# A gated recurrence and an attention of eight heads, laid between the matmuls of the projection before and the output after

## The chip, the cores and the metric

One core of a Trainium2 chip runs the whole program, once. TensorE multiplies, VectorE and ScalarE work on elements, GpSimd makes constants and issues small transfers, and SyncE issues the weight transfers. The metric is device microseconds of one launch, as the median of several runs.

## The reference, cut to what matters

Two transformer blocks of two layers each run over 256 tokens of width 1024, in float32. The change touches the first layer's mixer alone:

```
proj = hn @ w_in                       # 1024 -> 2568 columns
xr, yr, q, k, v, f_logit = split(proj) # 512 each, f_logit 8
xc = causal_conv(xr, width 4); r, i = sigmoid(block_diag(xc))
a = exp(-8 * r * softplus(-lam)); u = sqrt(1 - a*a) * (i * xc)
y_a = scan(h = a*h + u) * gelu(yr)
c = cumsum(log_sigmoid(f_logit + f_b))
y_b = causal_softmax(q k^T / 8 + c_i - c_j) v     # 8 heads of 64
h = h + concat(y_a, y_b) @ w_out
```

## The kernel before

All products of weights run as three float32r matmuls (high by high, high by low, low by high). A weight chunk of 128 x 1024 words lands in one of six slots of `raw_ring`; ScalarE copies its rounded high part (`split_hi`, L1263), VectorE subtracts for the low part (`split_lo`, L1699). `ahead(c)` on either engine splits up to three chunks (LEAD) beyond chunk c. A slot is reused once TensorE counts `chunk_used`, and a raw slot once `lo_ready` has passed. Activations stand in XHI and XLO, with 8 blocks of 128 rows.

The projection has 18 units, in the order of EV_COLS: sixteen "col" units (128 columns of the projection, 24 matmuls of 256 tokens), one "row" unit of 512 columns (V) and one of 8 (the forget logits); a row unit has 48 matmuls. `unit` waits for `bank_free` of the unit before last. VectorE evicts every unit.

Then the parameter rows, which GpSimd has loaded with 59 small transfers, are turned into columns, and `even_mixer` runs by itself: convolution on VectorE, gates on TensorE, sigmoid, exponential, tanh and square root on ScalarE, the scan on VectorE; then 16 attention units, unit v being head v // 2 and row block v % 2. In a unit TensorE makes scores (L875, L877), VectorE adds the bias and takes the maximum (L2054, L2056), ScalarE takes the exponential (L1490), VectorE scales (L2065, L2066), TensorE turns the probabilities (L888), ScalarE copies them (L1483) and TensorE multiplies by V (L894). Then `output` runs eight weight rows (L605), 12 matmuls of 512 columns each, and VectorE adds the residual (L1951).

Each engine executes its instructions in the order of the text; engines wait for each other by semaphores alone. The hybrid mixers of the second block (from about 1820 us) are already laid between column units.

## Time and profile before

| | |
|---|---|
| median of 3 runs | 2790.12 us |
| the three runs | 2780.39, 2792.97, 2790.12 us |
| profiled execution: time, span | 2793.78 us, 2792.0 us |
| mean granted TensorE clock | 0.942 of 2.4 GHz |
| busy share of the span: TensorE, VectorE, ScalarE, GpSimd | 93%, 69%, 52%, 2% |

The profile comes from one execution. Busy time counts instructions in execution, and idle time is given with the instruction that released the engine. A granted clock of 1.00 is 2.4 GHz for TensorE and 0.50 is 1.2 GHz.

### The profile page before, as it was taken

How to read it: one execution, taken by the hardware profiler on the slowest of the kernel's cores; microseconds unless marked ns; L12 is line 12 of the kernel's file. 1: busy time of each engine (PE TensorE's matmuls, PEld its weight loads, DVE VectorE, ACT ScalarE, POOL GpSimd, SP SyncE). 2: the span in 40 equal slices, each digit the busy share in tenths (PEclk: the TensorE clock that was granted, in tenths of full speed). 3: DMA queues.
4: the chain of work that ended last, by engine and by line, in shares of the span. 5: the costliest groups of instructions: out<-in, count | busy, mean ns of one | idle time of the engine just before them, and what ended most of it. 6: DMA issues, size and time to landing. Idle time of an engine off the chain costs nothing.

```text
span 2792.0 us, 40605 instructions
## 1 busy us (share of the span) xinstructions
PE 2600.0 (93%) x15264; PEld 2274.8 (81%) x15264; DVE 1940.5 (69%) x2674; ACT 1459.3 (52%) x1837; POOL 64.2 (2%) x137
## 2 busy tenths in 40 slices
PE   8589999669999999999999989989899899889998
PEld 8359997458888888888888779978799899787897
DVE  5445554448989898998999965578755555687654
ACT  4334442337777777777777743442443443523433
POOL 7000000000000000000000000000000000000000
PEclk9669998679999999999999999989999999989999
DMA  8026554119999999999999965621466556423463
GB/s 238 11 69 187 187 152 151 38 53 346 362 354 355 364 356 351 356 369 347 356 364 356 359 188 186 183 84 62 132 186 187 159 181 188 121 68 105 152 186 107
DMA packets 481892, 597.22 MB, mean 214 GB/s; under 512 B 21882, under 2 KB 313154, under 8 KB 481760
## 3 DMA queue, kind: packets, MB, share of 16 engines
q1 hardware_dynamic: 478048, 589.47, 62.7%
q0 software_dynamic: 3712, 6.00, 0.7%
q8 instruction: 81, 1.33, 0.2%
q14 instruction: 51, 0.42, 0.0%
HBM read 594.35 MB, written 1.05 MB: 213 GB/s over the span
## 4 chain that ended last, share of the span: by engine, by line
PE 88%; DVE 9%; ACT 2%; issue 1%; DMA 0%; SPq 0%; DVEq 0%; ACTq 0%
PE bank L622 23%; PE bank L779 23%; PE bank L805 11%; PE bank L634 11%; PE bank L585 6%; PE bank L582 2%; PE bank L605 2%; PE bank L848 2%; PE bank L1204 1%; PE bank L790 1%; DVE arena L2281 1%; PE bank L1020 1%; PE bank L726 1%; PE bank L950 0%; PE bank L877 0%
## 5 line engine op out<-in xcount | busy, mean ns | idle before, releaser
L1699 DVE TENSOR_TENSOR wlo_ring<-raw_ring,whi_ring 128x1024 fp32r<-128x1024 f32 x1122 | 1319.6, 1220 | 116.8 <-ACT whi_ring L1263 106.1
L1263 ACT CAST whi_ring<-raw_ring 128x1024 fp32r<-128x1024 f32 x1122 | 1141.3, 1052 | 290.3 <-DMA raw_ring<-in_od_exp_w_dram 155.8
L622 PE MATMUL bank<-xhi,whi_ring 128*128 128x256 f32 x1760 | 499.7, 284 | 0.4 <-DVE xlo L1756 0.4
L622 PE MATMUL bank<-xhi,wlo_ring 128*128 128x256 f32 x1760 | 499.0, 284 | 0.0
L622 PE MATMUL bank<-xlo,whi_ring 128*128 128x256 f32 x1760 | 499.0, 284 | 0.0
L622 PEld LDWEIGHTS bank<-xhi,whi_ring 128*128 128x128 f32 x1760 | 338.0, 192 | 4.7 <-issue 0.9
L622 PEld LDWEIGHTS bank<-xlo,whi_ring 128*128 128x128 f32 x1760 | 338.0, 192 | 3.9
L622 PEld LDWEIGHTS bank<-xhi,wlo_ring 128*128 128x128 f32 x1760 | 338.0, 192 | 0.0
L1792 DVE TENSOR_TENSOR hid<-sil,bank 128x256 f32<-128x256 f32 x110 | 46.4, 422 | 400.6 <-ACT sil L1324 400.6
L1324 ACT ACTIVATE sil<-bank 128x256 f32<-128x256 f32 x110 | 42.3, 385 | 499.1 <-PE bank L622 499.1
L779 PE MATMUL bank<-whi_ring,xg0hi 128*128 128x512 f32 x448 | 180.5, 403 | 1.2 <-issue 1.2
L779 PE MATMUL bank<-whi_ring,xg1hi 128*128 128x512 f32 x448 | 180.1, 402 | 0.0
L779 PE MATMUL bank<-whi_ring,xg1lo 128*128 128x512 f32 x448 | 177.5, 396 | 0.0
L779 PE MATMUL bank<-whi_ring,xg0lo 128*128 128x512 f32 x448 | 177.5, 396 | 0.0
L779 PE MATMUL bank<-wlo_ring,xg1hi 128*128 128x512 f32 x448 | 177.4, 396 | 0.0
L779 PE MATMUL bank<-wlo_ring,xg0hi 128*128 128x512 f32 x448 | 177.2, 396 | 0.0
L585 PE MATMUL bank<-xhi,whi_ring 128*128 128x256 f32 x496 | 150.7, 304 | 1.6 <-DVE xlo L1756 1.1
L585 PE MATMUL bank<-xlo,whi_ring 128*128 128x256 f32 x496 | 144.8, 292 | 0.0
L585 PE MATMUL bank<-xhi,wlo_ring 128*128 128x256 f32 x496 | 144.5, 291 | 0.0
L805 PE MATMUL bank<-whi_ring,hidhi 128*128 128x512 f32 x448 | 139.3, 393 | 1.4 <-DVE hidlo L1900 1.4
L805 PE MATMUL bank<-whi_ring,hidlo 128*128 128x512 f32 x448 | 138.6, 391 | 0.0
L805 PE MATMUL bank<-wlo_ring,hidhi 128*128 128x512 f32 x448 | 138.1, 390 | 0.0
(488 smaller groups left out, 3907.6 us busy)
## 6 DMA issues: line engine op xcount, KB each, us to landing
raw_ring<-in_od_exp_w_dram SPq DMA_DIRECT2D x672, 512.0 KB, 5.5
raw_ring<-in_ffn_w_gate_dram SPq DMA_DIRECT2D x88, 512.0 KB, 3.9
raw_ring<-in_ffn_w_up_dram SPq DMA_DIRECT2D x88, 512.0 KB, 5.5
raw_ring<-in_ffn_w_down_dram SPq DMA_DIRECT2D x88, 512.0 KB, 5.4
raw_ring<-in_ev_ffn_w_dram SPq DMA_DIRECT2D x66, 512.0 KB, 5.3
raw_ring<-in_w_in_dram SPq DMA_DIRECT2D x42, 512.0 KB, 4.0
raw_ring<-in_od_w_in_dram SPq DMA_DIRECT2D x24, 512.0 KB, 4.6
raw_ring<-in_ev_w_in_dram SPq DMA_DIRECT2D x20, 512.0 KB, 6.5
```

The source lines that it names most:

```text
L582: last = mm(row_bank(q, n, t), x[:, kt, t * P:(t + 1) * P], w[:, kk, :], start=st and (n > 256 or t == 0), stop=sp_, skip_group_check=True)
L585: last = mm(BANK[q % 2][:, 0:S], w[:, kk, :], x[:, kt, :], start=st, stop=sp_)
L605: last = mm(YB[t][h][:, :], x[:, kt, t * P:(t + 1) * P], w[:, h * 512:(h + 1) * 512], start=(kt == 0 and a == 0), stop=(kt == KT - 1 and a ...
L622: last = mm(BANK[qb][:, half * S:half * S + n], w[:, kt, :], x, start=(kt == 0 and a == 0), stop=(kt == KT - 1 and a == 2))
L634: last = mm(pair[h][:, :], x[:, b, t * P:(t + 1) * P], w[:, h * 512:(h + 1) * 512], start=(start and a == 0), stop=(stop and a == 2), skip ...
L779: last = mm(bank[:, :], x[:, kt, slots], w[:, kk, :], start=(kt == 0 and a == 0), stop=(kt == KT - 1 and a == 2))
L805: last = mm(BANK[4 + h][:, :], x[:, j * P:(j + 1) * P], w[:, h * 512:(h + 1) * 512], start=(g == 0 and j == 0 and a == 0), stop=(g == GROU ...
L848: last = mm(BANK[4 + b][:, (2 * j + t) * P:(2 * j + t + 1) * P], H[:, t, kt * P:(kt + 1) * P], DIAG[:, t, :], start=True, stop=True)
L1263: nc.scalar.copy(WHI[:, slot, 0:n], RAW[:, slot, 0:n]).then_inc(s["hi_ready"], 1)
L1324: af(SIL[:, b, 0:n], BANK[b][:, 0:n], ACT.Silu).then_inc(s["silu_ready"], 1)
L1699: V_.tensor_tensor(WLO[:, slot, 0:n], RAW[:, slot, 0:n], WHI[:, slot, 0:n].bitcast(F32), ALU.subtract)\
L1792: V_.tensor_tensor(HID[:, b, 0:n], SIL[:, qb, 0:n], BANK[qb][:, S:S + n], ALU.mult)\
```

## The change

The 8-column and the 512-column unit come first, then the four of XR, four of YR, and Q and K in turns. `even_mixer` now holds the projection and the output. On TensorE the sums of the forget gates stand after unit 5, the gates after unit 9, and the 16 attention units each follow a half of units 14 to 17 (steps 0 to 7) or a half of an output weight row (`out_part`, steps 8 to 15); the last rows follow. Values of unit v stand one step later. ScalarE evicts V, YR (with Gelu in the same operation), Q and K, and makes the high part of XHI; VectorE evicts the logits and XR, and does its recurrence operations between attention steps. GpSimd loads the rows that this mixer needs first, waits for them, and loads the others after; the constants are made in two parts.

The diff, cut to its core and shifted left by eight columns (Q's separate scaling, the old Gelu operations and the old loops leave):

```diff
-EV_COLS = [("col", P)] * 16 + [("row", 512), ("row", 8)]
+EV_XR, EV_YR, EV_Q, EV_K, EV_V, EV_FL = 0, 512, 1024, 1536, 2048, 2560
+EV_COLS = [("row", 8, EV_FL), ("row", 512, EV_V)] + [("col", P, x + P * i) for x in (EV_XR, EV_YR) for i in range(4)] \
+    + [("col", P, x + P * i) for i in range(4) for x in (EV_Q, EV_K)]
...
+FIRST_LOADS = sum(tile == 0 for tile, _ in row_at.values()) + 16 + 1
...
+    def load_rows(loads):
+        for dst, src in loads:
+            pool.dma_start(dst, src).then_inc(s["loads_done"], 16)
+    load_rows(row_loads[:FIRST_LOADS - 17])
+    pool.dma_start(FB[:, :], A["ev_f_b"].broadcast_to([P, 8])).then_inc(s["loads_done"], 16)
...
     link(nc.gpsimd.memset(ONES[:, :], 1.0))
     link(nc.gpsimd.memset(UPPER[:, :], 1.0))
+    link(nc.gpsimd.memset(CAUSAL[:, :], 0.0))
+    link(nc.gpsimd.memset(SEL[:, :, :], 1.0))
+    select(UPPER[:, :], ALU.is_ge, 0.0, [[1, P]], 0, -1)
+    select(SEL[:, :, :], ALU.is_equal, 0.0, [[1, 8], [0, P]], 0, -1)
+    nc.gpsimd.affine_select(out=CAUSAL[:, P:2 * P], in_=CAUSAL[:, P:2 * P], compare_op=ALU.is_ge, fill=NEG, base=0,
+                            pattern=[[-1, P]], channel_multiplier=1).then_inc(s["consts_ready"], 1)
+    pool.wait_ge(s["consts_ready"], 1)
+    pool.wait_ge(s["loads_done"], 16 * FIRST_LOADS)
+    load_rows(row_loads[FIRST_LOADS - 17:])
...
+    def even_mixer(pr, ou):
...
+        u(0)
+        u(1)
+        pe.wait_ge(s["loads_done"], 16 * FIRST_LOADS)
+        turn_columns(0, 1)
+        for k in range(2, 6):
+            u(k)
+        pe.wait_ge(s["consts_ready"], 1)
+        pe.wait_ge(s["small_ready"], 1)
...
+        mm(BANK[3][:, 8:16], UPPER[:, :], lf[:, 1, :], start=False, stop=True).then_inc(s["cum_ready"], 1)
+        for k in range(6, 10):
+            u(k)
+        pe.wait_ge(s["cols_ready"], 1)
         pe.wait_ge(s["conv_ready"], 1)
         for w, b in ((GA, 4), (GX, 6)):
...
         last.then_inc(s["gates_mm"], 1)
...
+        for k in range(10, 13):
+            u(k)
+        pe.wait_ge(s["loads_done"], 16 * N_LOADS)
+        pe.wait_ge(s["consts_ready"], 2)
+        pe.wait_ge(s["sig_ready"], 8)
+        turn_columns(1, 3)
+        u(13)
...
+        def out_part(kt, t):
+            c_ = ou["c0"] + kt
+            if t == 0:
+                wait(pe, "lo_ready", c_ + 1)
+                pe.wait_ge(s["x_ready"], x_at + kt + 1)
+            wh, wl = WHI[:, c_ % RING, :], WLO[:, c_ % RING, :]
+            for a, (x, w) in enumerate(((XHI, wh), (XHI, wl), (XLO, wh))):
+                for h in range(2):
+                    last = mm(YB[t][h][:, :], x[:, kt, t * P:(t + 1) * P], w[:, h * 512:(h + 1) * 512],
+                              start=(kt == 0 and a == 0), stop=(kt == KT - 1 and a == 2))
+            if t == TT - 1:
+                last.then_inc(s["chunk_used"], 1)
+            elif kt == KT - 1:
+                last.then_inc(s["y_ready"], 1)
...
+        def turn_probs(v):
+            t = v % 2
+            pe.wait_ge(s["probn_ready"], v + 1)
+            wait(pe, "probt_copied", v - 1 if v <= 8 else v)
+            bank = BANK[4 + t] if v < 8 else BANK[1]
...
+        def values(v):
...
+            pe.wait_ge(s["probt_copied"], v + 1)
+            if v == 12:
+                pe.wait_ge(s["x_ready"], x_at + 7)
+            bank = BANK[6 + h // 2] if v < 8 else BANK[0]
...
+        pe.wait_ge(s["cols_ready"], 2)
         scores(0)
         scores(1)
-        pe.wait_ge(s["sig_ready"], 8)
-        for u in range(16):
-            h, t = u // 2, u % 2
-            o = 64 * (h % 2)
-            pe.wait_ge(s["probn_ready"], u + 1)
-            wait(pe, "probt_copied", u - 1)
-            for b in range(t + 1):
-                last = tr(BANK[u % 2][:, b * P:(b + 1) * P], PR[:, u % 2, b * P:(b + 1) * P], IDENT[:, :])
-            last.then_inc(s["probt_ready"], 1)
-            if u + 2 < 16:
-                scores(u + 2)
-            pe.wait_ge(s["probt_copied"], u + 1)
-            for b in range(t + 1):
-                last = mm(BANK[4 + h // 2][o:o + 64, t * P:(t + 1) * P], V[:, b, h * 64:(h + 1) * 64],
-                          PT[:, u % 2, b, :], start=(b == 0), stop=(b == t))
-            last.then_inc(s["pv_ready"], 1)
+        for v in range(16):
+            if v < 8:
+                u(14 + v // 2, v % 2 * KT // 2, (v % 2 + 1) * KT // 2)
+            else:
+                if v == 8:
+                    pe.wait_ge(s["probt_copied"], 8)
+                if v == 12:
+                    pe.wait_ge(s["evhi_ready"], 6)
+                out_part((v - 8) % 4, (v - 8) // 4)
+            turn_probs(v)
...
+    def even_mixer(pr, ou):
...
+        def evict(u, dst, func, scale=1.0):
+            act.wait_ge(s["chunk_used"], c0 + u + 4)
+            act.wait_ge(s["bank_free"], q0 + u)
+            af(dst, BANK[(q0 + u) % 2][:, 0:S], func, scale=scale).then_inc(s["bank_free"], 1)
+        for i in range(5):
+            ahead(c0 + i)
+        act.wait_ge(s["chunk_used"], c0 + 5)
+        act.wait_ge(s["bank_free"], q0 + 1)
+        for t in range(TT):
+            last = nc.scalar.copy(V[:, t, :], row_bank(q0 + 1, 512, t))
+        last.then_inc(s["bank_free"], 1)
+        ahead(c0 + 5)
+        ahead(c0 + 6)
         act.wait_ge(s["spx_ready"], 1)
         af(SPE[:, :], SPN[:, :], ACT.Exp).then_inc(s["spe_ready"], 1)
+        ahead(c0 + 7)
+        ahead(c0 + 8)
+        for i in range(4):
+            ahead(c0 + 9 + i)
+            evict(6 + i, YR[:, i, :], ACT.Gelu_apprx_tanh)
...
         act.wait_ge(s["gates_mm"], 1)
...
+        ahead(c0 + 13)
+        evict(10, Q[:, 0, :], ACT.Copy, 64 ** -0.5)
...
         for i in range(4):
             af(AE[:, i, :], RG[:, i, :], ACT.Exp, scale=SPR[:, i:i + 1]).then_inc(s["aexp_ready"], 1)
+        ahead(c0 + 14)
+        evict(11, K[:, 0, :], ACT.Copy)
+        for i in range(4):
             af(TH[:, i, :], RG[:, i, :], ACT.Tanh, scale=SPS[:, i:i + 1]).then_inc(s["aexp_ready"], 1)
+        ahead(c0 + 15)
+        evict(12, Q[:, 1, :], ACT.Copy, 64 ** -0.5)
+        ahead(c0 + 16)
         act.wait_ge(s["root_in"], 1)
         af(TH[:, :, :], TH[:, :, :], ACT.Sqrt).then_inc(s["root_ready"], 1)
...
+        evict(13, K[:, 1, :], ACT.Copy)
+        ahead(c0 + 17)
+        def hi(kt, src):
+            nc.scalar.copy(XHI[:, kt, :], src).then_inc(s["evhi_ready"], 1)
...
+        exps(0)
+        exps(1)
+        for v in range(16):
+            if v < 8 and v % 2:
+                ahead(c0 + 17 + v // 2)
+                u = 14 + v // 2
+                if u % 2 == 0:
+                    evict(u, Q[:, u // 2 - 5, :], ACT.Copy, 64 ** -0.5)
+                else:
+                    evict(u, K[:, u // 2 - 5, :], ACT.Copy)
+            if v == 5:
+                act.wait_ge(s["pv_ready"], 4)
+                nc.scalar.copy(PVS[:, 0, :], BANK[6][:, 0:S])
+            if v == 8:
+                act.wait_ge(s["lru_ready"], 1)
+                hi(0, YR[:, 0, :])
+            copy(v)
+            if v + 2 < 16:
+                exps(v + 2)
+            if v == 7:
+                act.wait_ge(s["chunk_used"], c0 + 21)
+            if v == 8:
+                for kt in range(1, 4):
+                    hi(kt, YR[:, kt, :])
+                act.wait_ge(s["pv_ready"], 8)
+                nc.scalar.copy(PVS[:, 1, :], BANK[7][:, 0:S])
+                ahead(oc)
+            if v == 9:
+                act.wait_ge(s["lru_ready"], 1)
+                hi(4, PVS[:, 0, :])
+                hi(5, PVS[:, 1, :])
+                ahead(oc + 1)
+            if v == 10:
+                ahead(oc + 2)
+            if v == 12:
+                act.wait_ge(s["pv_ready"], 12)
+                hi(6, BANK[0][:, 0:S])
+            if v in (13, 14, 15):
+                ahead(oc + v - 10)
+        ahead(oc + 6)
+        act.wait_ge(s["pv_ready"], 16)
+        hi(7, BANK[0][:, 0:S])
+        ahead(oc + 7)
+        load_root()
...
+    def even_mixer(pr, ou):
...
+        def evict(u, dst):
+            ahead(c0 + u + 3)
+            dve.wait_ge(s["chunk_used"], c0 + u + 4)
+            dve.wait_ge(s["bank_free"], q0 + u)
+            V_.tensor_copy(dst, BANK[(q0 + u) % 2][:, 0:S]).then_inc(s["bank_free"], 1)
+        ahead(c0)
+        dve.wait_ge(s["chunk_used"], c0 + 1)
+        V_.tensor_copy(flat_(FL), BANK[q0 % 2][:, 0:16]).then_inc(s["bank_free"], 1)
...
+        for i in range(1, 5):
+            ahead(c0 + i)
+        dve.wait_ge(s["cols_tp"], 1)
+        V_.tensor_copy(COLS[:, 0, :], BANK[6][:, 0:P]).then_inc(s["cols_ready"], 1)
+        dve.wait_ge(s["cols_ready"], 1)
...
+        evict(2, XR[:, 0, 4:S + 4])
+        evict(3, XR[:, 1, 4:S + 4])
+        ahead(c0 + 7)
         dve.wait_ge(s["spe_ready"], 1)
         log1p(SP[:, :], SPE[:, :], SPP[:, :], SPR[:, :], SPS[:, :])
...
+        evict(4, XR[:, 2, 4:S + 4])
+        evict(5, XR[:, 3, 4:S + 4])
+        dve.wait_ge(s["bank_free"], q0 + 6)
         for j in range(4):
+            ahead(c0 + 9 + j)
...
+        ahead(c0 + 14)
         dve.wait_ge(s["sig_ready"], 8)
         link(V_.tensor_tensor(flat_(IG), flat_(IG), flat_(XC), ALU.mult))
+        ahead(c0 + 15)
+        dve.wait_ge(s["aexp_ready"], 4)
+        link(V_.tensor_tensor(flat_(RG), flat_(AE), flat_(AE), ALU.mult))
+        dve.wait_ge(s["cols_tp"], 2)
+        for t in (1, 2):
+            last = V_.tensor_copy(COLS[:, t, :], BANK[6 - t][:, 0:P])
+        last.then_inc(s["cols_ready"], 1)
+        dve.wait_ge(s["cols_ready"], 2)
         dve.wait_ge(s["aexp_ready"], 8)
-        link(V_.tensor_tensor(flat_(RG), flat_(AE), flat_(AE), ALU.mult))
         V_.scalar_tensor_tensor(flat_(TH), flat_(RG), 1.0, flat_(TH), ALU.add, ALU.mult)\
             .then_inc(s["root_in"], 1)
...
+        ahead(c0 + 16)
+        ahead(c0 + 17)
...
+        def lo(kt, src):
+            dve.wait_ge(s["evhi_ready"], kt + 1)
+            V_.tensor_tensor(XLO[:, kt, :], src, XHI[:, kt, :].bitcast(F32), ALU.subtract)\
+                .then_inc(s["x_ready"], 1)
+        logits(0)
+        logits(1)
+        for v in range(16):
+            normed(v)
+            if v + 2 < 16:
+                logits(v + 2)
+            if v == 1:
+                dve.wait_ge(s["root_ready"], 1)
+                link(V_.tensor_tensor(flat_(IG), flat_(IG), flat_(TH), ALU.mult))
+            if v == 2:
+                for i in range(4):
+                    last = V_.tensor_tensor_scan(XC[:, i, :], AE[:, i, :], IG[:, i, :], 0.0, ALU.mult, ALU.add)
+                link(last)
+            if v == 3:
+                dve.wait_ge(s["bank_free"], q0 + 10)
+                V_.tensor_tensor(flat_(YR), flat_(YR), flat_(XC), ALU.mult).then_inc(s["lru_ready"], 1)
+                dve.wait_ge(s["lru_ready"], 1)
+            if v < 8 and v % 2:
+                ahead(c0 + 17 + v // 2)
+            if v == 7:
+                lo(0, YR[:, 0, :])
+            if v == 8:
+                for kt in range(1, 4):
+                    lo(kt, YR[:, kt, :])
+                ahead(oc)
+            if v == 9:
+                lo(4, PVS[:, 0, :])
+                lo(5, PVS[:, 1, :])
+                ahead(oc + 1)
+            if v == 10:
+                ahead(oc + 2)
+            if v == 12:
+                lo(6, BANK[0][:, 0:S])
+            if v in (13, 14, 15):
+                ahead(oc + v - 10)
+        ahead(oc + 6)
+        lo(7, BANK[0][:, 0:S])
+        ahead(oc + 7)
```

## Rows read from the trace of the kernel before

**Rows 1.** Windows by stage: width, busy of each engine, granted clock, DMA share.

```profile
13.80:78.00 64.20, 63.19 (x481) 61.13 (x482) 36.15 (x49) 22.95 (x27) 37.37 (x75) 0.99 0.76 215
78.00:117.40 39.40, 10.35 (x40) 7.29 (x39) 22.76 (x58) 16.63 (x28) 0.00 (x0) 0.59 0.00 1
117.40:176.60 59.20, 48.80 (x128) 25.71 (x128) 21.39 (x73) 15.63 (x50) 0.00 (x0) 0.50 0.00 0
176.60:200.60 24.00, 23.53 (x92) 19.25 (x92) 9.97 (x11) 7.79 (x9) 2.01 (x3) 0.87 0.66 200
```

**Rows 2.** Chain that ended last, first 260 us: start, length, what.

```profile
18.08 43.45 PE bank L585 x360
...
200.57 1.23 DVE h L1951
```

**Rows 3.** Waits between 78 and 177 us: who for whom, total, times, longest.

```profile
DVE arena L2054 <- PE bank L877: 35.7, 14, 3.1
PE bank L888 <- DVE arena L2066: 23.0, 15, 16.0
```

**Rows 4.** Timeline of TensorE over one head: start, busy, instruction.

```profile
122.58 0.69 PE L888 MATMUL bank<-ident,arena 128*128 128x128 f32 x2 [0.60 <-DVE arena L2066]
123.20 1.22 PE L875 MATMUL bank<-arena 64*128 64x256 f32 x2
...
125.49 1.11 PE L894 MATMUL bank<-arena 128*64 128x128 f32 x4
126.99 0.47 PE L888 MATMUL bank<-ident,arena 128*128 128x128 f32 x1 [0.38 <-DVE arena L2066]
...
128.83 0.69 PE L894 MATMUL bank<-arena 128*64 128x128 f32 x2
```

**Rows 5.** Windows of the projection's last two units, columns as in rows 1.

```profile
61.50:72.30 10.80, 10.80 (x50) 8.91 (x49) 4.05 (x5) 3.16 (x3) 0.00 (x0) 1.00 0.63 238
72.30:78.00 5.70, 5.70 (x50) 5.70 (x49) 2.42 (x3) 0.00 (x0) 0.00 (x0) 0.93 0.31 90
```

**Rows 6.** Timeline of TensorE after the recurrence's gates.

```profile
102.11 0.70 PE L875 MATMUL bank<-arena 64*128 64x256 f32 x2
102.73 0.48 PE L877 MATMUL bank<-arena,sel 8*128 8x256 f32 x1
```

**Rows 7.** Costliest groups of the page: busy, mean ns, idle before.

```profile
L1699 DVE TENSOR_TENSOR wlo_ring<-raw_ring,whi_ring 128x1024 fp32r<-128x1024 f32 x1122 | 1319.6, 1220 | 116.8 <-ACT whi_ring L1263 106.1
L1263 ACT CAST whi_ring<-raw_ring 128x1024 fp32r<-128x1024 f32 x1122 | 1141.3, 1052 | 290.3 <-DMA raw_ring<-in_od_exp_w_dram 155.8
```

**Rows 8.** Timeline of VectorE in recurrence and attention.

```profile
87.97 5.09 DVE L2022 SCALAR_TENSOR_TENSOR arena<-arena,cols 128x256 f32<-128x256 f32 x12
...
111.74 2.44 DVE L2043 TENSOR_TENSOR_SCAN arena<-arena 128x256 f32<-128x256 f32 x4
...
121.39 0.35 DVE L2054 SCALAR_TENSOR_TENSOR arena<-bank,arena,causal 128x128 f32<-128x128 f32 x1 [2.07 <-PE bank L877]
121.78 0.29 DVE L2056 TENSOR_REDUCE arena<-arena 128x1 f32<-128x128 f32 x1
...
122.17 0.35 DVE L2066 TENSOR_SCALAR arena<-arena 128x256 f32<-128x256 f32 x1
```

**Rows 9.** Timeline of ScalarE in recurrence and attention.

```profile
99.14 3.02 ACT L1466 ACTIVATE arena<-bank,cols 128x256 f32<-128x256 f32 x8 [15.10 <-PE bank L857]
...
118.11 0.40 ACT L1490 ACTIVATE arena<-arena 128x128 f32<-128x128 f32 x1 [3.72 <-DVE arena L2056]
```

**Rows 10.** Windows in the later mixer that is woven already.

```profile
1867.00:1869.00 2.00, 0.50 (x5) 0.29 (x3) 1.39 (x3) 0.00 (x0) 0.00 (x0) 1.00 0.07 22
1869.00:1871.00 2.00, 0.00 (x0) 0.00 (x0) 1.93 (x5) 0.00 (x0) 0.00 (x0) 1.00 0.00 0
1873.00:1875.00 2.00, 2.00 (x13) 1.76 (x12) 0.88 (x2) 0.00 (x0) 0.00 (x0) 0.50 0.60 166
```

**Rows 11.** Timeline of GpSimd's transfers.

```profile
29.58 4.14 POOL L456 DMA_DIRECT2D arena<-in_ev_gx_w_dram  x8
```

More of the change, by code:

```diff
@@ L257, in build @@
         AMX, ASUM, AREC = c(16), c(16), c(16)
+        PVS = c(2, S)
         c = Carve()
@@ new lines, in scores @@
+                def scores(v):
+                    h, t = v // 2, v % 2
+                    o, n = 64 * (h % 2), (t + 1) * P
+                    wait(pe, "logit_ready", v - 1)
+                    wait(pe, "bank_free", pr["q0"] + 12 + 2 * (h // 2))
+                    mm(BANK[2 + v % 2][:, 0:n], Q[o:o + 64, h // 2, t * P:(t + 1) * P], K[o:o + 64, h // 2, 0:n],
+                       start=True, stop=False)
+                    mm(BANK[2 + v % 2][:, 0:n], SEL[:, h, :], NCT[:, 0:n], start=False, stop=True)\
+                        .then_inc(s["score_ready"], 1)
@@ L898, in odd_mixer @@
+                out_part(4, 0)
+                values(15)
+                out_part(4, 1)
+                for kt in range(5, KT):
+                    for t in range(TT):
+                        out_part(kt, t)
             def odd_mixer():
@@ L1215, in _ @@
             turn_norm()
-            project(EV_PROJ)
-            pe.wait_ge(s["consts_ready"], 1)
-            pe.wait_ge(s["loads_done"], 16 * N_LOADS)
-            for t in range(3):
-                last = tr(BANK[5 + t][:, 0:P], ROWS[:, t, :], IDENT[:, :])
-            last.then_inc(s["cols_tp"], 1)
-            pe.wait_ge(s["cols_ready"], 1)
-            even_mixer()
-            output(EV_OUT)
+            even_mixer(EV_PROJ, EV_OUT)
             turn_norm()
@@ new lines, in exps @@
+                def exps(v):
+                    n = (v % 2 + 1) * P
+                    act.wait_ge(s["logit_ready"], v + 1)
+                    wait(act, "probt_ready", v - 1)
+                    af(PR[:, v % 2, 0:n], LG[:, v % 2, 0:n], ACT.Exp, bias=AMX[:, v:v + 1],
+                       accum_out=ASUM[:, v:v + 1]).then_inc(s["prob_ready"], 1)
+                exps(0)
[37 more added lines that the diff above has]
+                        ahead(oc + v - 10)
@@ L1644, in _ @@
             gain("norm_mix0")
-            project(EV_PROJ)
-            act.wait_ge(s["cols_ready"], 1)
-            even_mixer()
-            output(EV_OUT)
+            even_mixer(EV_PROJ, EV_OUT)
             norm()
@@ L2068, in even_mixer, with normed @@
-                for p in range(4):
-                    dve.wait_ge(s["pv_ready"], 4 * p + 4)
-                    split_x(BANK[4 + p][:, 0:S], 4 + p, 5 + p, 1)
+                def normed(v):
+                    n = (v % 2 + 1) * P
+                    dve.wait_ge(s["prob_ready"], v + 1)
+                    link(V_.reciprocal(AREC[:, v:v + 1], ASUM[:, v:v + 1]))
+                    V_.tensor_scalar(PR[:, v % 2, 0:n], PR[:, v % 2, 0:n], AREC[:, v:v + 1], None, ALU.mult)\
+                        .then_inc(s["probn_ready"], 1)
@@ L2472, in _ @@
             gain("norm_mix0")
-            project(EV_PROJ, ev_dest)
-            dve.wait_ge(s["cols_tp"], 1)
-            for t in range(3):
-                last = V_.tensor_copy(COLS[:, t, :], BANK[5 + t][:, 0:P])
-            last.then_inc(s["cols_ready"], 1)
-            dve.wait_ge(s["cols_ready"], 1)
-            even_mixer()
-            output(EV_OUT)
+            even_mixer(EV_PROJ, EV_OUT)
             residual(EV_OUT)
```

122 lines of the change are left out of this document (45 added, 77 removed).

## The prediction

> **What bounds the kernel now.** I read the windows by stage first, because the change touches only the first 200 us. The stretch from 13.8 to 200.6 us has four stages [rows 1]: the projection's 18 units, where TensorE works 63.2 of 64.2 us at a granted clock of 0.99; the recurrence (78.0 to 117.4), where it works 10.35 of 39.4 us at 0.59; the attention (117.4 to 176.6), 48.8 of 59.2 us at 0.50; the output, 24.0 us at 0.87. The chain that ended last runs through the projection's matmuls and leaves this layer with VectorE's residual sum at 200.57 [rows 2]. Everything after 200.6 keeps its code, so the kernel's time moves by what 200.57 moves.
>
> The waits of the middle stretch show why TensorE is slow there [rows 3]: VectorE waits 35.7 us in 14 times for scores, TensorE 23.0 us for normalised probabilities (16.0 of it the first). The engines hand one tile round. One head takes 7.4 us (59.2 over 8 [rows 1]) and contains 4.02 us (second row block: 122.58 to 126.60) plus 2.53 us (first: 126.99 to 129.52) of TensorE work, 6.55 us, all at the lower clock [rows 4]. So two things can be won: the waits, if TensorE has other matmuls, and the half clock, if that keeps it granted at full (2.4 GHz instead of 1.2).
>
> **The work that stays.** Nothing large is removed. The projection's units keep 63.2 us of TensorE [rows 1]; a 512-column unit is 10.8 us, the 8-column one 5.7 us [rows 5], and a column unit 24 matmuls of 0.121 us (43.45 us for 360 [rows 2]), 2.9 us. The output at full clock: its window has 24 us at mean 0.87, which is 6.2 us at half and the rest at full; 23.5 us less the 3.1 lost is 20.4 us, 1.28 us for each of 16 new half rows. Attention at full clock: a pair for 256 score columns takes 0.62 us at full (102.11 to 102.73 [rows 6]) and 1.15 at half (two pairs, 123.20 to 125.49 [rows 4]), a ratio of 0.54. Transposes and values have no row at full clock; bounds are 0.5 (the clocks' ratio) and 1.0 of their low-clock time, and I take 0.54, from the matmul beside them in the same head. So 8 x 6.55 x 0.54 = 28.3 us (26.2 to 52.4). Gates, sums and column turns: 10.35 less about 2.0 for the first scores, 8.3 us at mixed clock, 4.9 if all were full (8.3 x 0.59); I take 6.4. Sum of TensorE work: 63.2 + 6.4 + 28.3 + 20.4 = 118.3 us.
>
> **Waits before the first probabilities: 7.9 us.** A split of a weight chunk costs ScalarE 1.05 and VectorE 1.22 us [rows 7]; both queues are executed in order, so each split stands in front of attention or recurrence work.
> - Convolution: four column units hide it. Its 16 operations take 6.5 us (12 in 5.09 [rows 8]) and stand between four splits of which each follows a Gelu eviction on ScalarE, so it can end only after the split that follows unit 8, plus 1.22 and 1.7: about 1.5 us after unit 9.
> - Column turns, second part: TensorE has four column units and two turns after the gates, 12.0 us. ScalarE in that time does sigmoids 3.0 [rows 9], splits, evictions, exponentials and a tanh group; VectorE's split 18 ends about 12.9 us after the gates, then one product (1.2) and two copies (0.5): 14.6. TensorE waits 2.5 us for cols_ready 2.
> - First probabilities: after it, VectorE has a product and two splits, then logits, exponential and scaling, 7.3 us, against scores 0 and 1 and a half unit, 3.4 us: 3.9 us of wait.
>
> **The sixteen steps: 22 us of waits.** TensorE's order in a step is half unit (1.44) or half row (1.28), turn, scores(v+2), values(v-1). From scores(v+2) to the turn of v+2 the chain is logits 0.6 or 0.9 (0.35 + 0.29 at 128 columns), exponential 0.4 plus its sum read (0.6 to 0.7), scaling 0.35 plus a reciprocal, 0.5 [rows 8, 9]: about 2.1 us, against some 6 us of TensorE's work in the two steps between. Bare, the weave has slack. The waits come from what VectorE has in front of normed(v). Steps 0 to 7: 0.9 at step 2 (product 1.2), 1.5 at step 3 (four scans 2.44 [rows 8]), 2.1 at step 4 (product and split), 0.9 at step 6 (split): 5.4. Steps 8 to 15, where three queues take turns at XHI, XLO and the splits: at 8, 2.3 (logits(9), exponential, then hi(0) on ScalarE and lo(0) on VectorE); at 9, 1.5 and 2.2; at 10, 3.6; at 11, 2.2; at 13, 0.7; at 14, 2.9; at 15, 1.1: 16.5. The largest as the pattern: from the end of scores(11), logits 0.9, exponential 0.7, hi(4) and hi(5) 0.7, ScalarE's split 1.05, VectorE's 1.22, normed(10) 0.5 and handovers are 5.3 us; TensorE has values(8) and a half row, 1.7. The smaller ones go the same way: at 9, the four parts of XHI and XLO, 0.4 us each, and one split on both queues stand before normed(9), while TensorE has one half row; at 14 and 15 a split on both queues stands before normed. Together 22 us; bounds 0 (all hidden) and about 44, where each wait is doubled by the other queue.
>
> **The clock: 10 us.** The 8-column unit moves from last to first. In its old place its 5.7 us window averages 0.93 [rows 5], so the clock fell 4.9 us after it began; only 0.8 us was lost then. Now the 512-column unit stands behind it. Low for as long as in the output stage (6.2 us, above) costs 3.1, with the tail of the unit itself 3.8 us (bounds 0 and 5.7 + 3.1). In the steps, the later mixer, which is woven in this way already, shows what a pause does: its window 1867 to 1869 has 0.5 us of matmuls, the next none, both at 1.00, and 1873 to 1875 is full of matmuls at 0.50 [rows 10]. Two of my waits (3.9 and 3.6) are of that size; two low stretches like the output's cost 6.2 us (bounds 0 and what rival 2 gives).
>
> **Moved to other queues, at nothing.** GpSimd issues a transfer each 0.52 us (8 in 4.14 [rows 11]). In front of TensorE's first parameter wait now stand 15 rows, 1 bias and 16 gate blocks: 32 x 0.52 from 2.5 us is 19 to 20 us; the wait is after unit 1, beyond 30 us. The 27 left follow and are wanted only after unit 12. The cover gone, each microsecond late is one of the kernel's. Evictions of YR, Q and K go to ScalarE at 0.33 to 0.4 us each, beside matmuls; the separate scaling of Q and Gelu's four operations leave. SyncE's order of chunks changes only within the projection, and weights of 2 KB rows come first, so the 0.8 us wait near 17.3 us should go (in the 1.0 us idle of [rows 1]; not counted).
>
> **Sum.** 13.8 + 118.3 + 7.9 + 22.0 + 3.8 + 6.2 = 172.0 us for the end of the output, against 200.6: 28.6 us less. The profiled execution took 2793.8 us (span 2792.0), so it becomes 2765; it lies 3.7 above the median of the three runs, so from 2790.1 I predict 2761.5, rounded to 2762.
>
> **Rivals.**
> 1. *Tighter than I count.* The waits of steps 8 to 15 shrink, since work that waits is not late for two reasons at once, and no low stretch follows. For it: the later mixer stays at 1.00 in most windows with such gaps. Against: in-order queues leave no slack at steps 9 and 10. 38 to 48 us less: about 2747.
> 2. *The clock stays low through the sixteen steps.* Attention with 48.8 of 59.2 us busy was never granted more than half [rows 1]. For it: that row; against: now half of TensorE's time is the dense matmuls beside which the clock was full. Work of the steps at half: 52.4 + 23.0 (eight half units) + 20.5 (eight half rows) = 96 us, some 4 of waits, 10.2 of rows left: 110. My sum has 85 from the first turn on: 26.2 of attention (the first two scores are before it), 10.1 of half units, 20.4, 22.0 and 6.2. 25 of the 28.6 us are given back: about 2787.
> 3. *Slower.* As 2, but the waits remain beside the low clock (22 instead of 4) and the last rows are low too (20.4): 138 against 85, 53 us more, 24 slower than before: about 2815. It decides once the steps lose 43 us against my sum.
> 4. *The parameters land late*, or the weave fails to cover at all: price 1 for 1, no row speaks for it.
>
> The Trainium skill (TensorE: Matmul & The Clock Gate, section "HAM oscillation — how this bites in real kernels") speaks against this change: it tells of bursts of matmuls with pauses between, after each of which the array starts again at the low clock. By that rule every step would be like the old attention, and the time would be rival 2's. The trace agrees for one long pause [rows 10] and no row shows a weave of attention.
>
> **How the numbers follow.** Forecast (20 to 37 us less) 0.59; rival 1 0.13; between forecast and rival 2 (14 to 20 less) 0.11; rival 2 (within 14) 0.13; rival 3 and late parameters 0.04. 0.5% is 14 us, about what can be told from no change here (the three runs spread 12.6 us). Faster 0.83, same 0.13, slower 0.04. The range 2746 to 2780 leaves out the better end of rival 1 and the worse of rivals 2 and 3.
>
> **What would show it.** Right: the output's last matmul at 165 to 180 us; nearly all of TensorE busy until 72 us, with half clock for a few microseconds near 20; waits for cols and the first probabilities near 75 to 87; larger waits in the half-row steps than in the half-unit steps, released by VectorE's scaling; ScalarE and VectorE below 70% there. Wrong: 0.50 clock from 80 us on (rival 2), a wait of over 2 us on GpSimd's transfers near 32 us, or waits in steps 8 to 15 outside 8 to 30 us.

## The result, and the profile after

The changed kernel took 2766.16 us (median of 4 runs, 2760.41 to 2771.41), the kernel before 2791.55 us beside it (4 runs). The ratio is 0.9912, 95% interval 0.9886 to 0.9939: faster by 0.9%, about 25 us. Run again it took 2761.02 us (median of 6 runs), ratio 0.9886 (0.9866 to 0.9906). The prediction was 2762. Two launches far outside all others, one of 6461 us (e1 below) and one of 8083 us (the kernel before, beside e4 to e7), are left out of the ratios.

The profiled execution took 2768.26 us (span 2766.5 us, mean granted clock 0.949; before 2793.78, 2792.0 and 0.942). First the windows of the span that the change touches (columns as in [rows 1]):

```profile
13.80:72.00 58.20, 55.61 (x382) 51.92 (x382) 34.80 (x69) 27.96 (x43) 36.32 (x76) 0.94 0.64 167
72.00:90.00 18.00, 14.84 (x73) 11.99 (x73) 11.57 (x19) 11.41 (x22) 0.00 (x0) 0.72 0.35 119
90.00:110.00 20.00, 17.47 (x79) 12.93 (x80) 10.66 (x23) 5.75 (x16) 0.00 (x0) 0.75 0.09 27
110.00:130.00 20.00, 15.00 (x75) 10.06 (x73) 9.57 (x23) 7.65 (x22) 0.00 (x0) 0.93 0.17 53
130.00:150.00 20.00, 18.56 (x56) 11.29 (x56) 7.67 (x19) 6.21 (x17) 0.00 (x0) 0.64 0.28 79
150.00:172.00 22.00, 19.39 (x79) 13.31 (x78) 8.77 (x17) 8.30 (x13) 2.00 (x3) 0.92 0.43 128
```

TensorE is busy for 141 of 158 us, where it was busy for 146 of 187 [rows 1]. The granted clock, which was 0.59 in the recurrence and 0.50 in the attention, now goes up and down between the levels. The first residual sum on VectorE, which ends this layer's mixer:

```profile
171.92 2.58 DVE L2090 TENSOR_TENSOR h<-h,bank 128x1024 f32<-128x1024 f32 x2 [4.44 <-PE bank L910]
```

It stands at 171.92 us, 28.65 before the 200.57 of [rows 2]; the prediction said 172.0. TensorE's timeline shows each place where it still waits before this point, in brackets how long and for whom (L876 sums the forget gates, L888 are the recurrence's gates, L922 scores, L933 turns the probabilities, L910 is a half weight row):

```profile
45.78 0.38 PE L876 MATMUL bank<-upper,arena 128*8 128x128 f32 x2 [1.05 <-DVE arena L2171]
...
60.51 1.75 PE L888 MATMUL bank<-arena 128*128 128x256 f32 x7 [1.54 <-DVE arena L2183]
...
78.34 0.46 PE L922 MATMUL bank<-arena 64*128 64x128 f32 x2 [2.42 <-issue]
...
84.93 0.47 PE L933 MATMUL bank<-ident,arena 128*128 128x128 f32 x1 [0.74 <-DVE arena L2224]
...
93.86 0.33 PE L933 MATMUL bank<-ident,arena 128*128 128x128 f32 x1 [0.69 <-DVE arena L2224]
98.71 0.44 PE L933 MATMUL bank<-ident,arena 128*128 128x128 f32 x2 [1.50 <-DVE arena L2224]
...
104.66 0.47 PE L933 MATMUL bank<-ident,arena 128*128 128x128 f32 x1 [0.34 <-DVE arena L2224]
...
121.81 0.70 PE L910 MATMUL bank<-whi_ring,xhi 128*128 128x512 f32 x2 [2.23 <-DVE xlo L2229]
...
126.52 0.70 PE L910 MATMUL bank<-whi_ring,xhi 128*128 128x512 f32 x2 [1.55 <-DVE xlo L2229]
...
129.52 0.69 PE L933 MATMUL bank<-ident,arena 128*128 128x128 f32 x2 [0.64 <-DVE arena L2224]
...
137.37 0.48 PE L933 MATMUL bank<-ident,arena 128*128 128x128 f32 x1 [1.39 <-DVE arena L2224]
...
156.65 0.33 PE L933 MATMUL bank<-ident,arena 128*128 128x128 f32 x1 [2.31 <-DVE arena L2224]
```

Two waits of 0.58 (step 6) and 0.30 us (step 13) complete the list: 1.05, 1.54, 2.42 and 0.74 us before the first probabilities, and 3.1 us in steps 0 to 7 and 8.4 in steps 8 to 15. At the "issue" of 78.34 the engine's queue stood at `cols_ready` 2. That is 17.3 us of waits in all. Not all of them are for the attention's chain: 3.8 us, in front of the first two half rows, are for XLO's parts (L2229). In windows of 1 us the clock stands at half at 18 to 24.8, 79.4 to 89.6, 99.9 to 110, 127 to 144.1 and 157.9 to 161.3 us: 47.8 us, 41.0 of them in the steps.

GpSimd's last gate block, issued at its old rate and now in front of the constants, is issued by 20.5 us. GpSimd itself waits for it and goes on at 25.8 us, and TensorE shows no wait for it after unit 1 at 33 us:

```profile
16.39 4.14 POOL L463 DMA_DIRECT2D arena<-in_ev_gx_w_dram  x8
...
25.84 0.57 POOL L455 DMA_DIRECT2D rows<-in_sc_conv_w_dram  x1 [0.58 <-DMA arena<-in_ev_gx_w_dram]
```

Of the 28.65 us, 25.5 arrive at the end. The residual sums after each mixer keep their distance, to 0.4 us, until 2372.6 us (2400.9 before); the second block's later hybrid mixer then takes 185.2 us instead of 182.4. It has the same instructions. Its windows, before:

```profile
2403.00:2586.00 183.00, 162.08 (x1242) 148.91 (x1242) 143.24 (x295) 68.67 (x112) 0.00 (x0) 0.90 0.28 85
```

and after:

```profile
2375.00:2558.00 183.00, 165.12 (x1242) 151.25 (x1242) 140.63 (x290) 67.28 (x108) 0.00 (x0) 0.88 0.29 85
```

The same 1242 matmuls are 3 us longer at a mean clock of 0.88 instead of 0.90. The second profile of the same changed kernel has 182.4 us for this mixer again (2370.2 to 2552.6), so the 2.8 us belong to this execution and not to the change.

### The profile page after: what moved, and what is told of

Read it like the earlier page. It is cut to its first block, busy times and chain, and to the rows that moved or that the text cites. A ratio compares the mean times of both kernels' runs of the same rounds, so it can differ in the third digit from the quotient of the medians.

```text
span 2766.5 us, 40654 instructions
## 1 busy us (share of the span) xinstructions
PE 2598.6 (94%) x15264; PEld 2275.1 (82%) x15264; DVE 1931.3 (70%) x2656; ACT 1464.0 (53%) x1857; POOL 62.8 (2%) x137
## 3 DMA queue, kind: packets, MB, share of 16 engines
HBM read 594.35 MB, written 1.05 MB: 215 GB/s over the span
## 4 chain that ended last, share of the span: by engine, by line
PE 88%; DVE 9%; ACT 2%; issue 1%; DMA 0%; DVEq 0%; SPq 0%; ACTq 0%
PE bank L626 23%; PE bank L783 23%; PE bank L809 11%; PE bank L638 11%; PE bank L589 5%; PE bank L586 3%; PE bank L852 2%; PE bank L1279 1%; PE bank L794 1%; DVE arena L2480 1%; DVE wlo_ring L1838 1%; PE bank L609 1%; PE bank L1095 1%; PE bank L730 1%; PE bank L910 1%
## 5 line engine op out<-in xcount | busy, mean ns | idle before, releaser
L1838 DVE TENSOR_TENSOR wlo_ring<-raw_ring,whi_ring 128x1024 fp32r<-128x1024 f32 (+1 forms) x1122 | 1317.9, 1218 | 134.4 <-ACT whi_ring L1330 123.2
L1330 ACT CAST whi_ring<-raw_ring 128x1024 fp32r<-128x1024 f32 (+1 forms) x1122 | 1140.7, 1052 | 254.3 <-DMA raw_ring<-in_od_exp_w_dram 154.5
```

The source lines that it names most:

```text
L1330: nc.scalar.copy(WHI[:, slot, 0:n], RAW[:, slot, 0:n]).then_inc(s["hi_ready"], 1)
L1838: V_.tensor_tensor(WLO[:, slot, 0:n], RAW[:, slot, 0:n], WHI[:, slot, 0:n].bitcast(F32), ALU.subtract)\
```

## Experiments

All ratios are to the kernel before, with the 95% interval. "End" is the start of the first residual sum, in us; waits are the sum of TensorE's waits of over 0.4 us from 13 us to the end; half clock is the time at half clock, counted in windows of 1 us.

| kernel | median us | ratio | end | waits | half clock |
|---|---|---|---|---|---|
| the change, first profile | 2766.16 | 0.9912 (0.9886 to 0.9939) | 171.92 | 16.6 | 47.8 |
| e0_after_again | 2761.02 | 0.9886 (0.9866 to 0.9906) | 169.64 | 16.6 | 40.9 |
| e1_extras_late | 2746.83 | 0.9831 (0.9812 to 0.9851) | 155.81 | 10.0 | 27.3 |
| e2_logits_col | 2753.83 | 0.9847 (0.9828 to 0.9866) | 171.73 | 14.7 | 58.0 |
| e3_filler | 2766.09 | 0.9900 (0.9879 to 0.9920) | 173.6 | 17.2 | 41.0 |
| e4_params_old | 2759.47 | 0.9876 (0.9847 to 0.9905) | 173.10 | 19.3 | 44.4 |
| e5_attention_bare | 2778.87 | 0.9959 (0.9943 to 0.9975) | 190.45 | 30.9 | 85 |
| e6_both | 2742.45 | 0.9822 (0.9800 to 0.9844) | 149.36 | 10.1 | 17.1 |
| e7_early_hi | 2739.53 | 0.9820 (0.9797 to 0.9844) | 146.63 | 7.2 | 17.1 |
| e7_again | 2735.37 | 0.9793 (0.9767 to 0.9820) | 142.22 | 6.9 | 6.8 |
| e8_early_logits | 2738.53 | 0.9806 (0.9780 to 0.9832) | 145.29 | 5.7 | 17.1 |

The runs come from three chips: e0 to e3 on one, e4 to e7 on the second, e7_again and e8 on the third. An end is one execution's, with that execution's clock: where it and the median disagree, the median decides.

**The change again (e0).** No edit.

> The changed kernel again, as the anchor for the three others on this chip. Expected: end of the output (first residual sum on VectorE) at 172 us again, span 2760 to 2770 us, the same stretches at half clock (about 18 to 25, 79 to 90, 100 to 110, 127 to 144, 158 to 161 us). If the granted clock of these stretches is a matter of chance, they move by several microseconds and the end of the output with them.

The waits have the same sum to 0.1 us, though single ones differ (step 10: 2.92 us against 1.39), and the stretches at half clock lie elsewhere (19 to 23, 77 to 84, 97 to 108, 118 to 129, 135 to 142, 155 to 160), 6.9 us less of them, and the output ends 2.3 us sooner. The places expected for them were missed, as the expectation's second half allowed. So an end has a spread of a few us from the clock alone.

**Which half of the weave pays (e5).** The attention is taken out of the weave; the recurrence stays between the column units.

```diff
-                u(13)
+                for k in range(13, 18):
+                    u(k)
...
                 for v in range(16):
-                    if v < 8:
-                        u(14 + v // 2, v % 2 * KT // 2, (v % 2 + 1) * KT // 2)
-                    else:
-                        ...
-                        out_part((v - 8) % 4, (v - 8) // 4)
                     turn_probs(v)
```

> The recurrence stays between the column units, but units 14 to 17 run before the attention and all sixteen half rows after it. This splits the gain. Theory: most of the gain comes from the recurrence, which left TensorE idle for 29 of 39.4 us, and the attention bare costs its old 59 us at half clock, at most 6 us of which the weave hides, so the output ends near 180 to 188 us (15 to 20 of the 28.7 us are kept). Rival: the weave of the attention carries half or more of the gain; then the end is at 186 us or later (under 15 us kept), and the clock is at 0.50 from the first scores to 5 us after the last.

Ten runs give 0.41% below before, 11 us; the full change has 0.9 to 1.1%. So the recurrence beside the units is worth about 11 us and the attention's weave the other 13 to 20. The end, 190.45 us, is outside the 180 to 188 of the theory: the rival was right, the attention's weave carries more than half. The attention's windows, and some of its timeline:

```profile
95.00:171.00 76.00, 50.17 (x134) 27.04 (x135) 28.59 (x76) 18.91 (x59) 0.00 (x0) 0.51 0.07 21
171.00:190.00 19.00, 19.00 (x85) 15.73 (x84) 6.13 (x6) 6.73 (x7) 2.00 (x3) 1.00 0.49 144
...
120.00:127.40 7.40, 6.41 (x18) 3.46 (x17) 2.32 (x8) 1.73 (x6) 0.00 (x0) 0.50 0.00 0
```

Bare attention stays at half from 95 to 171 us, also in a head where TensorE is busy for 6.41 of 7.40 us, and the dense output behind it has 1.00 at once. Low clock in bare attention is thus not removed by starting it right behind units at full clock. Taking the units from between also brought waits back (30.9 us in all), so this run alone does not part the two.

**What the waits in the steps are (e1).** VectorE's recurrence products, scans, weight splits and XLO parts of step v, which stood between `logits(v + 2)` and `normed(v + 1)`, now follow `normed(v + 1)`: the scaling for which TensorE waits is in front of them.

```diff
                 for v in range(16):
                     normed(v)
+                    if v:
+                        extras(v - 1)
                     if v + 2 < 16:
                         logits(v + 2)
-                    if v == 1:
-                        dve.wait_ge(s["root_ready"], 1)
-                        ...
+                extras(15)
```

> VectorE's side work of a step (products, scans, XLO parts, chunk splits) stands behind the next step's scaling instead of in front of it. Queue theory: the side work in front of the scaling makes TensorE's waits, and the waits make the low clock. Then the waits of steps 2, 3, 9, 10, 14 fall to under 0.5 us each, the low stretches after 99 us shrink by half or more, and the output ends at 160 to 166 us instead of 171.9. Rival, clock theory: the attention's own matmuls bring the clock down whatever the waits; then TensorE's waits fall but 30 us or more stay at half clock, and the output ends at 168 to 171 us.

14 us by the medians against e0 (13.8 by the ends, more than the theory's 6 to 12). Waits of every length shrink by 7.5 us, and the half clock, counted only where TensorE is busy, costs 6.0 us less: 13.5 together. Of the waits in the steps 0.93 (the first probabilities), 2.62, 1.55 and 0.46 us are left, and with the others two falls of the clock are gone. One execution alone would not show that, since the falls move by themselves; but the five profiles with the old order on VectorE and woven attention (the change, e0, e2, e3, e4) all have a fall between 97 and 104 us, behind a wait of 1.5 to 1.8 us, and one between 155 and 160, behind the 2.31 us of step 14. The five with the new order (e1, e6, e7 twice, e8) have no fall between the stretch at the first steps and the half rows, and none in the last 20 us. The windows, and two steps of the timeline at full clock:

```profile
72.00:92.00 20.00, 16.66 (x86) 13.59 (x85) 11.57 (x19) 13.29 (x26) 0.00 (x0) 0.74 0.39 131
92.00:115.00 23.00, 20.91 (x128) 15.60 (x127) 16.19 (x38) 9.90 (x28) 0.00 (x0) 1.00 0.15 46
115.00:156.00 41.00, 38.36 (x156) 26.28 (x157) 20.04 (x45) 17.08 (x38) 2.00 (x3) 0.92 0.41 121
```

```profile
94.55 0.27 PE L933 MATMUL bank<-ident,arena 128*128 128x128 f32 x1
...
95.58 0.65 PE L944 MATMUL bank<-arena 128*64 128x128 f32 x4
...
97.69 0.38 PE L933 MATMUL bank<-ident,arena 128*128 128x128 f32 x2
...
99.25 0.43 PE L944 MATMUL bank<-arena 128*64 128x128 f32 x2
```

Here attention woven with units and without waits has the full clock for 23 us. One head then costs TensorE 1.68 (94.55 to 96.23) plus 1.99 us (97.69 to 99.68) = 3.67 us, where the prediction took 6.55 x 0.54 = 3.54. The largest waits that remain in the steps are the 2.6 and 1.5 us for XHI and XLO in front of the first two half rows.

**The logits as a column unit (e2).** The 8-column row unit has 48 matmuls whose moving side is 8 columns; as a column unit it has 24 of 256 tokens, and two small transposes bring the result back.

```diff
-EV_COLS = [("row", 8, EV_FL), ("row", 512, EV_V)] + ...
+EV_COLS = [("col", 8, EV_FL), ("row", 512, EV_V)] + ...
...
+                    if first == 0:
+                        pe.wait_ge(s["bank_free"], pr["q0"] + 1)
+                        for t in range(TT):
+                            tr(BANK[6][:, P + 8 * t:P + 8 * t + 8], NCT[:, t * P:(t + 1) * P], IDENT[0:8, 0:8])
```

> The eight forget logits are computed as a column unit (24 matmuls of 256 tokens with 8 weight columns, 2.9 us) instead of a row unit (48 matmuls of 8 columns, 5.7 us), and turned by two small transposes. If the 8-column matmuls bring the clock down at 18 us, no window before 30 us is at 0.50, the 512-column unit ends near 28 us instead of 33.1, and the output ends 5 to 6 us earlier, near 166. Rival: the clock falls for another reason (the start itself), then only 1 to 2.5 us are gained, since the 512-column unit also needs VectorE's split, done near 17.2 us.

7 us by the medians. The window 13.8 to 20, at 0.83 before this edit, is now at full clock:

```profile
13.80:20.00 6.20, 5.58 (x34) 3.54 (x33) 6.09 (x12) 4.76 (x7) 6.20 (x14) 1.00 0.67 163
72.00:97.00 25.00, 24.23 (x83) 17.83 (x83) 12.98 (x29) 9.42 (x22) 0.00 (x0) 0.52 0.19 63
```

The gates start at 54.93 us instead of 58.88 (e0), 4 us sooner. So the first half of the theory holds, no half clock before 30 us; the end near 166 us did not come. This profile's end does not show the 4 us, since 72 to 97 us fell to half (58.0 us in all); its profiled launch was also the slowest of the five, 2764.92 us. That stretch begins behind the wait of 2.43 us, as in the change, but then lasts 24 us, with TensorE busy for 24.23 of 25 us and no further wait over 0.25 us. So woven matmuls without waits can also stay at half for long; what brings the clock back was not found.

**Filling one wait (e3).** Ten extra matmuls of 512 columns, whose results nobody reads, stand in the wait for `cols_ready` 2.

```diff
+                for i in range(10):
+                    mm(BANK[7][:, :], XHI[:, i % 4, 0:P], XHI[:, 4:6, :], start=True, stop=True)
                 pe.wait_ge(s["cols_ready"], 2)
```

> Ten matmuls of 512 columns whose result nobody reads (2.2 us) are put into TensorE's wait of 2.4 us at 76 us. If the pause is what brings the clock down at 79.4 us, the stretch 79 to 90 us stays at 1.00 and the output ends 3 to 5 us earlier (the last step's wait for the first probabilities, 0.7 us now, grows to 3 to 4 and takes part of it back). Rival: the attention's own matmuls or the next wait bring it down; then a stretch of 8 us or more at half clock still begins between 79 and 85 us and the end moves by less than 1.5 us.

No gain. The wait of 2.4 us is filled, but the first turn then meets a wait of 2.85 us for the first probabilities (0.74 in the change), and the clock falls behind that one, for 3.4 us (87 to 92) instead of 10.2:

```profile
86.70 0.33 PE L933 MATMUL bank<-ident,arena 128*128 128x128 f32 x1 [2.85 <-DVE arena L2226]
```

The chain over VectorE sets this point; work on TensorE in front of it does not shorten it. TensorE's idle time up to the end is 17.7 us, as in e0 (17.6), and the fillers add 2.5 us of work. Neither expectation held to the letter: the fall was shorter and later than the rival said, and the stretches at half were 41.0 us in all, as in e0, 10.2 of them at the start and 17.1 from 135 us.

**The order of the parameters (e4).** All 59 transfers are issued and awaited at once, as before.

```diff
-            load_rows(row_loads[:FIRST_LOADS - 17])
+            load_rows(row_loads)
...
-                pe.wait_ge(s["loads_done"], 16 * FIRST_LOADS)
+                pe.wait_ge(s["loads_done"], 16 * N_LOADS)
```

> All 43 row transfers, the bias and the 16 gate blocks are issued before TensorE's first parameter wait, as in the kernel before, and nothing after. Theory (the order of the transfers is part of the gain): the last is issued near 34 us and lands near 38, so TensorE waits 4 to 5.5 us after the 512-column unit (33.1 us now), the constants come 6 us after the transfers, and the output ends 5 to 9 us later than 170 to 172 us. Rival: the wait only replaces the other waits of the recurrence (units 2 to 9 have slack), and the end moves by less than 2 us.

TensorE waits where the change does not:

```profile
35.96 0.33 PE L863 MATMUL bank<-ident,rows 128*128 128x128 f32 x1 [2.40 <-DMA arena<-in_ev_gx_w_dram]
```

and the wait at the small sums shrinks to 0.38 us (1.05 in the change, 0.47 in e0). The theory had 4 to 5.5 us for the first. TensorE is idle for 20.4 us up to the end, against 17.6 in e0, so the old order costs 2.8 us of waits in this profile. The times do not show it: 0.9876, with four runs, against 0.9912 and 0.9886 of the change. A gain from this part of the change was not measured.

**Both, and the next waits (e6, e7, e8).** e6 is e1 and e2 together.

> VectorE's side work behind the next scaling and the eight logits as a column unit, together. Queue theory: the two act at different places and add, so the output ends 5 us before that of the first alone (155.8 us, which had 10.3 us at half clock near 16 to 27 us), near 150 us, and the time is 18 to 22 us below the changed kernel's. Rival: what the logits' unit gives is lost again in the granted clock later (its own trace had 58 us at half clock in total), and the sum is no better than 14 us.

e7 makes XHI and XLO of rows 0 and 1 in step 7, one step earlier.

```diff
-                    if v == 8:
+                    if v == 7:
                         act.wait_ge(s["lru_ready"], 1)
                         hi(0, YR[:, 0, :])
+                        hi(1, YR[:, 1, :])
```

> As the one with both, and the first two parts of XHI and XLO are made in step 7, directly after the projection's last read of XHI, the next two in step 8. If the queue order makes the waits of 2.6 and 1.6 us at the first half rows, both vanish, no low stretch begins there, and the output ends 4 to 7 us earlier than in the one with both. Rival: the parts now delay the copies and exponentials of step 7, the wait moves to the turn of step 8 or 9, and the end moves by less than 1.5 us.

> Edit: none against e7_early_hi; it is the anchor for e8_early_logits on the same chip. Theory: 2739 us within 3, the output's end within 3 us of 146.6, the half-clock stretches at other places than in the first profile of it. Rival: if the stretches at half clock are fixed by the code, they stand at the same places (74 to 86 and 109 to 116).

In e8 VectorE copies the columns first and then makes the product and the root's input; the split that stood in front follows, and the next two go behind the scalings of steps 1 and 2. ScalarE makes one split behind the first two exponentials.

```diff
-                ahead(c0 + 15)
-                dve.wait_ge(s["aexp_ready"], 4)
-                link(V_.tensor_tensor(flat_(RG), flat_(AE), flat_(AE), ALU.mult))
...
+                link(V_.tensor_tensor(flat_(RG), flat_(AE), flat_(AE), ALU.mult))
...
-                ahead(c0 + 16)
-                ahead(c0 + 17)
+                ahead(c0 + 15)
...
+                    if v < 2:
+                        ahead(c0 + 16 + v)
```

> Edit: the kernel of e7_early_hi, and in it the first logits come earlier on VectorE's and ScalarE's queues: the column copies and the root's input stand before the splits of the values, and two of the splits move into the first two steps. Theory (what is left of the waits for the columns, 2.44 us at 71, and for the first probabilities, 1.05 us at 79, is a queue and not arithmetic; and the half clock of 74 to 86 begins behind that wait): both waits together shrink by 1.5 to 3 us, the output ends 3 to 5 us before the 146.6 us of e7_early_hi, near 142 to 144, and the kernel takes about 2736 us. Rival (the scaling and the exponentials are only moved, and the clock's falls do not follow these waits): the output ends within 1.5 us of 146.6 and the time stays at 2739 or above.

e6: 0.9822, against 0.9831 and 0.9847 of its parts; its end, 149.36 us, and its 18 us below the changed kernel are what the theory said. Against e1 alone it is 4.4 us lower by the medians, from two chips.

e7 is 2.9 us below e6 by the medians of the same chip, with ranges that overlap (2736.93 to 2747.62 and 2738.11 to 2744.17 us), and its end is 2.7 us sooner: less than the 4 to 7 of its theory. The two waits shrank from 2.62 and 1.56 us to one of 1.09, and in its first profile a stretch at half still begins there. In e7_again the end was 4.4 us sooner than in the first profile, beyond the 3 us expected; the stretch at 73 to 81 us is there again, the one at 109 to 116 is not.

e8 is 3.2 us above e7_again on the same chip, and the ranges do not overlap. The wait of 2.44 us for the columns is gone and a wait of 1.99 us for the first probabilities begins 3.6 us later (74.49 against 70.86 us): most of that wait was only moved, as the rival said. TensorE is idle for 1.2 us less in all; what the profile of e8 has more is half clock, 17.1 against 6.8 us, the same 17.1 as in e7's first profile. So e8 gained nothing. Whether it is really the slower one is open: e7's two ratios, 0.9793 and 0.9820, lie on both sides of e8's 0.9806, with intervals that overlap. e7_again has the lowest median, 2735.37 us. Its windows in the second run:

```profile
16.00:73.00 57.00, 52.65 (x377) 48.66 (x375) 38.44 (x71) 31.89 (x48) 36.59 (x71) 1.00 0.65 174
73.00:81.00 8.00, 7.64 (x25) 5.28 (x25) 5.50 (x10) 4.91 (x9) 0.00 (x0) 0.57 0.51 183
81.00:142.00 61.00, 58.68 (x299) 41.61 (x298) 37.10 (x84) 28.16 (x70) 2.01 (x3) 1.00 0.32 96
```

From 81 us to the end the clock is 1.00, with TensorE busy for 58.68 of 61 us. From e0 to here TensorE's idle time shrinks by 10.3 us, what the half clock costs while it is busy by 15.7, and its work by 1.5: 27.5 us, where the ends are 27.4 apart.

## Why the prediction was right, point by point

The sum was right to 0.1 us at the end of the output, by two errors that cancel: the waits were put 12.6 us too high and the clock 12.3 us too low. The two are linked, as shown below, but that they are of one size is luck. The term that was mis-sized most is the clock in the steps (6.2 us predicted, 18.9 found).

- **The work: right.** 118.3 us predicted, 118.5 found. From 13.8 to 172.0 us TensorE is busy for 140.9 us; of the 47.8 us at half clock it waited 3.1 and was busy 44.7, and half of these, 22.3, is what the clock cost. With the waits, 13.8 + 118.5 + 17.3 + 22.3 = 171.9. The attention's ratio of 0.54, taken from one pair of matmuls, gave 3.54 us for a head and e1 shows 3.67.
- **Waits before the first probabilities: 7.9 predicted, 5.8 found.** Convolution 1.5 (found 1.54) and column turns 2.5 (2.42) were right. The first probabilities were put at 3.9 and cost 0.74: the half unit ran at half clock from 79.4 us and covered them. In e3, where the clock was still full, the same wait is 2.85, so 3.9 was about 1 us too much as well. And 1.05 us at the small sums was not foreseen: `small_ready` waits for log1p on VectorE, behind its splits.
- **Waits in the steps: 22.0 predicted, 11.5 found; the term mis-sized.** The pattern is right: half-row steps have 8.4 of the 11.5, and steps 3 (1.5 predicted, 1.50) and 8 (2.3, 2.23) meet their numbers; 14 (2.9, 2.31) is near. At step 9 the wait for the parts is 1.55 (1.5), the one for the scaling 0.64 instead of 2.2. Steps 4, 10, 11 and 15 (2.1, 3.6, 2.2, 1.1) came to 0.3, 1.4, 0 and 0. All of these stand in or just behind stretches at half clock, where TensorE's own work took up to twice the time against which the chain on VectorE was laid. The same prices at full clock were not measured for all steps.
- **The clock: 10.0 predicted, 22.3 found; the term mis-sized.** The start cost 3.4 (3.8 predicted). In the steps two low stretches of the output stage's length were assumed; there were four, of 10.2, 10.2, 17.1 and 3.4 us, 18.9 us lost on TensorE's work instead of 6.2. The prediction costed a step's waits at full clock and then added the clock, so it let both errors cover each other: a low stretch pays in part with waits that it removes.
- **The rivals.** Rival 1 had the smaller waits and no low stretch; the change had the first half only. With the waits removed as well, e7 took 2735 and 2740 us, below its 2747. Rival 2 is partly true: 41 of the 94 us from the first scores to the residual sum were at half. That the clock must stay low through all sixteen steps, however woven, is refuted by e1 (92 to 115 us at 1.00) and e7_again (81 to 142); that removed waits are enough to keep it at full is not shown, since e2 stayed at half for 24 us without them. Its price was also too high by about 5 us: its 110 counts all scores and eight half units at half clock, where the 85 beside it leaves out the first two scores and the first half unit. Rival 3 needed 43 us of loss in the steps, and there were 12.7 more of clock and 10.5 less of waits. Rival 4 fell: the first 32 transfers were issued by 20.5 us, as said, and had landed by 25.8, before TensorE wanted them at 33.
- **What the trace was to show.** The last output matmul ends at 173.2 us, the waits are larger in the half-row steps, ScalarE and VectorE are below 70%: as said. The 8.4 us of waits in steps 8 to 15 lie at the lower edge of the 8 to 30 named, and 3.8 of them were released by XLO's parts, not by the scaling.

The Trainium skill (TensorE: Matmul & The Clock Gate, section "HAM oscillation — how this bites in real kernels") tells of a kernel that waits for a transfer behind each short burst of matmuls and starts each next burst at the low clock. Those waits are longer than any in this weave; the prediction took from it that every step would be like the old attention, which is more than the page says. The traces agree in part, and already with shorter waits: the falls at 79 and 99 us stand right behind waits of 2.42 and 1.50 us, and the second went when e1 took the waits of steps 2 and 3 away. But the wait of 1.54 us at 59 us, between dense units, is followed by no fall, in this or any other profile here.

## What to carry to other kernels

Before weaving a chain between dense matmuls, write down for each step what stands on the feeding engine between "input ready" and "result wanted"; put side work behind the wanted result, not in front of it. That order alone was worth 14 us here, about half of what the whole weave gave (25 to 32). Where a wait and a low clock are both expected, do not add them as if apart: the low clock covers waits, and removing the waits gave back both here. A wait filled with other matmuls is not a wait removed.

## What the runs showed of the hardware

- The same code with the same waits does not have the same clock. Timelines and windows of e7's two profiles, the first:

```profile
107.89 0.70 PE L914 MATMUL bank<-whi_ring,xhi 128*128 128x512 f32 x2 [1.09 <-DVE xlo L2234]
```

```profile
109.00:116.00 7.00, 7.00 (x21) 4.62 (x20) 3.66 (x8) 2.79 (x8) 0.00 (x0) 0.51 0.25 75
```

and the second:

```profile
105.56 0.70 PE L914 MATMUL bank<-whi_ring,xhi 128*128 128x512 f32 x2 [1.09 <-DVE xlo L2234]
```

```profile
109.00:116.00 7.00, 6.33 (x29) 3.89 (x27) 4.57 (x12) 4.87 (x13) 0.00 (x0) 1.00 0.49 141
```

After the same wait of 1.09 us one execution falls to half for 7 us and the other does not. Why is open. It makes one profile's end uncertain by 2 to 5 us here.
- Bare attention stays at half also where TensorE is busy for 6.41 of 7.40 us (e5), while a weave with 20.91 of 23 us busy holds 1.00 (e1) and another, with 24.23 of 25, stays at half (e2). Which property of the small matmuls does it was not tried by itself.
- With the 8-column row unit first, all six profiles (the change, e0, e1, e3, e4, e5) have 3.4 to 10.3 us at half clock between 16 and 27 us; with the column unit in its place, none of the five (e2, e6, e7 twice, e8) has any before 72 us. The column unit is also shorter, so which of its properties does it is open.
